# Latent-attention heads: the rotary query channels of two heads in one product

## Chip, core and metric

One NeuronCore of a Trainium2 chip runs the whole kernel. The metric is the device time of one execution in microseconds (us).

## What is computed

One encoder layer over 512 tokens of 2048 channels, in float32: a mixer with two attention branches, then a mixture of 16 experts. The change concerns the latent-attention branch (8 heads). Cut to it:

```python
q = (_rmsnorm(cq, g_cq) @ w_uq).reshape(b, s, MLA_HEADS, MLA_NOPE_DIM + MLA_ROPE_DIM)   # 8 heads x (128 + 64)
qn, qr = q[..., :MLA_NOPE_DIM], _rope(q[..., MLA_NOPE_DIM:], ang_1d)
kv = (_rmsnorm(ckv, g_ckv) @ w_ukv).reshape(b, s, MLA_HEADS, MLA_NOPE_DIM + MLA_V_DIM)
kr = _rope(kr, ang_1d)                                # one rotary key, shared by the heads
s = (einsum(qn, kn) + einsum(qr, kr)) * scale
p = softmax(s);  o = p @ v

def _rope(x, ang):                                    # x1, x2: halves of 32 channels
    return concatenate([x1 * cos - x2 * sin, x1 * sin + x2 * cos])
```

## The kernel before

Engines are programmed separately and meet in semaphores; the order on each engine is written out by hand. Stages, in order: adaLN columns and the combined input projection, the gate projections, **attention** (about 646 to 870 us of the profile), the two branch projections, the output projection, the experts. In attention one loop runs over `i` = 0..7; each turn does latent head `i` and grouped-query head `i+1` (the latter is called attention `2i+2`, latent head `i` is attention `2i+1`; `a` counts both).

Products are exact to float32 by splitting both operands in a rounded part (`_hi`, type fp32r, made by ACT) and a rest (`_lo`, made by DVE): `split_product` (L902) issues hi*hi, lo*hi and hi*lo. A product over the 512-channel latent with 128 output channels and 512 tokens is thus 4 x 3 = 12 matmuls of 512 columns.

Turn `i` on PE (L1002 to L1025): `project(i)` makes the head's rotary queries in bank 5 (12 matmuls), its other queries in bank 4 (12) and its keys in bank 7 (6); on even `i` `values_two` makes the values of two heads in banks 6 and 5, two token tiles in each; on `i` = 3 the second grouped-query key head is transposed into bank 5. Then `rope_scores` (12 matmuls into banks 0 to 3), two transpositions of the probabilities of attention `2i`, `nope_scores` (12 more into the same banks), the transposition of the next grouped-query queries into bank 5, and the rest of attention `2i` and, between its parts, the scores of attention `2i+2` and the values of `2i+1`.

The rotary queries of one head take 128 columns because each of its 64 channels is wanted twice: the weights stand as [q1 q2 | q2 q1] (`uq` is 256 wide, `wq` is loaded with two extra strips of 32 columns, L580 and L581), the table `qtab` holds [cos cos -sin sin], one multiplication on DVE over 128 rows (L2106) turns the bank, and the keys stand twice under one another (`kr2`, L1994), so that the product over 128 rows adds the two halves.

```python
for b, w0, turn in ((5, P, 1), (4, 0, 2)):            # L918: rotary queries, then the others
    split_product(bank[b][:, :], by_k(4, lambda k: three(uq_hi[:, k, w0:w0 + P], ...)), True, True)
k[:, C_QTAB:C_QTAB + S] = np.concatenate([c1.T, c1.T, -s1.T, s1.T])   # L103
```

ACT's turn: the copy of the previous latent head's output (`output_hi`), `head_inputs(i)` (L1591: `qr_hi`, `qn_hi`, `kn_hi`, on even `i` the values), the weights of head `i+1` (`head_uq_hi`, `head_ukv_hi`), three exponentials, `item_hi`, the fourth, the normalisation of the probabilities (L1583), and the same for attention `2i+2`. DVE's turn: `output_lo`, `head_rests(i)` (L2103: the turning, then `qr_lo`, `qn_lo`, `kn_lo`), the weight rests, the copies `pT` of transposed probabilities (L2101) with the negative maxima of the scores (L2082, L2084) between them. `inverse_sums` waits for the four exponentials. On `i` = 7 the next head's weights are replaced by the first two chunks of the branch weights (`hi(N_BR, 0)`, `hi(N_BR + 1, 1)` on ACT, L1622, and `lo` on DVE, L2129); these use the memory that holds `uq`, `uk` and `uv` during attention.

The SP queue loads the head weights (L578): four transfers per head, heads 0 and 1 at the start, head `H` as soon as DVE has split head `H-2`. PE's `project(i)` waits for the rests of its weights (`hw_lo`), for `o_lo` before bank 4 and for `pT_ready` before bank 7.

## Time and profile before

| | us |
|---|---|
| median of 3 runs (lowest to highest) | 2217.11 (2216.94 to 2217.76) |
| the profiled execution, device time | 2216.92 |
| its span, first to last instruction | 2214.6 |
| attention in it, first scores to first branch product | 646.5 to 869.5 |

The span leaves out some 2.3 us around the program. PE is TensorE's matmuls, PEld its weight loads, DVE VectorE, ACT ScalarE, SP the queue that issues the loads. A matmul row merges matmuls of one kind that follow each other; as they are pipelined, the distance of two rows' starts, not the row's length, is what the first costs. In brackets stands the idle time before a row and who ended it.

### The profile page before, as it was taken

The page shows a single profiled execution, that of the slowest core. Times are in us where ns is not written, and L with a number is a line of the kernel's source. Part 1 is how long each engine was busy: PE and PEld are TensorE (multiplying, and loading weights), DVE is VectorE, ACT ScalarE, POOL GpSimd, SP SyncE. Part 2 cuts the span into 40 slices and gives each one's busy share as a digit, 9 for nine tenths or more (in the row PEclk, how much of TensorE's full clock was granted, in tenths as well). Part 3 has the DMA queues.
Part 4 walks back from the last instruction along what each step waited for, and adds up shares of the span by engine and source line. Part 5 has one row for each costly group of instructions (what it writes and reads, how often), then busy time and mean ns, then how long its engine had stood idle before and what let it go on. Part 6 is the DMA issues. An engine that isn't in the chain of part 4 may idle for free.

```text
span 2214.6 us, 26365 instructions
## 1 busy us (share of the span) xinstructions
PE 2124.1 (96%) x10338; PEld 1380.8 (62%) x10338; DVE 871.9 (39%) x1229; ACT 566.4 (26%) x996; POOL 4.7 (0%) x8
## 2 busy tenths in 40 slices
PE   7999999999999999999999899999999999998996
PEld 4777788888887767888888545343534444444432
DVE  4572667666666665445433400202030202121114
ACT  4254442222246664212222511010100000100102
POOL 0000000000000000000000000000000000000000
PEclk9999999999999999999999999999999999999999
DMA  9966775888770100543422699999999999999998
GB/s 335 338 228 248 270 252 169 319 314 288 276 236 26 29 15 1 190 154 130 158 94 76 273 390 425 390 427 427 426 428 429 426 428 426 428 427 426 427 423 309
DMA packets 150319, 635.61 MB, mean 287 GB/s; under 512 B 20418, under 2 KB 33880, under 8 KB 119012
## 3 DMA queue, kind: packets, MB, share of 16 engines
q1 hardware_dynamic: 145636, 626.18, 72.0%
q10 hardware_dynamic: 4608, 8.39, 1.0%
q8 instruction: 52, 0.85, 0.2%
q14 instruction: 23, 0.19, 0.0%
HBM read 621.94 MB, written 12.58 MB: 287 GB/s over the span
## 4 chain that ended last, share of the span: by engine, by line
PE 84%; DMA 8%; DVE 4%; ACT 1%; SPq 1%; issue 1%; DVEq 0%; ACTq 0%
PE bank L1219 25%; PE bank L744 24%; PE bank L746 13%; DMA e_wide<-in_w_e_up 6%; PE bank L1191 5%; PE bank L905 4%; PE bank L794 3%; PE bank L991 2%; PE bank L1211 2%; PE bank L1212 1%; DMA e_slot<-in_w_e_down 1%; PE bank L1201 1%; PE bank L713 1%; PE bank L979 1%; DMA sh_tile<-in_w_ada 1%
## 5 line engine op out<-in xcount | busy, mean ns | idle before, releaser
L1219 PE MATMUL bank<-e_wide,xgT 128*64 128x512 f32 x1456 | 405.5, 603 | 42.8 <-DMA e_slot<-in_w_e_up 16.3
L1398 ACT ACTIVATE w_hi<-stage 128x1024 fp32r<-128x1024 f32 (+1 forms) x168 | 175.3, 1044 | 600.7 <-PE bank L744 339.9
L1801 DVE TENSOR_TENSOR w_lo<-stage,w_hi 128x1024 fp32r<-128x1024 f32 (+1 forms) x168 | 202.4, 1205 | 313.9 <-ACT w_hi L1398 313.2
L1219 PEld LDWEIGHTS bank<-e_wide,xgT 128*64 128x64 f32 x1456 | 129.0, 139 | 292.1 <-issue 289.6
L1219 PE MATMUL bank<-e_slot,xgT 128*64 128x512 f32 x584 | 213.1, 610 | 0.0
L1219 PE MATMUL bank<-e_wide,heT 128*64 128x512 f32 x672 | 168.7, 595 | 0.0
L744 PE MATMUL bank<-hT_hi,w_hi 128*128 128x512 f32 x512 | 159.2, 392 | 0.0
L744 PE MATMUL bank<-hT_lo,w_hi 128*128 128x512 f32 x512 | 158.0, 390 | 0.0
L744 PE MATMUL bank<-hT_hi,w_lo 128*128 128x512 f32 x512 | 157.8, 389 | 0.0
L1872 DVE SCALAR_TENSOR_TENSOR ada_acc<-ada_tile,siluc,ada_acc 128x1024 f32<-128x1024 f32 x116 | 148.7, 1282 | 6.7 <-DMA ada_tile<-in_w_ada 1.2
L2334 DVE TENSOR_TENSOR x<-x,bank 128x512 f32<-128x512 f32 x128 | 79.6, 683 | 175.3 <-PE bank L1212 173.8
L2324 DVE SCALAR_TENSOR_TENSOR y<-bank,val,gt_row 128x512 f32<-128x512 f32 x32 | 22.0, 745 | 318.4 <-PE bank L1219 318.4
L1723 ACT ACTIVATE xgT<-bank,modcol,a 128x128 f32<-128x128 f32 x112 | 42.1, 456 | 402.7 <-PE bank L1191 402.7
L1219 PEld LDWEIGHTS bank<-e_wide,heT 128*64 128x64 f32 x672 | 52.9, 137 | 101.5 <-issue 99.4
L1191 PEld LDWEIGHTS bank<-sel,xn 128*128 128x128 f32 x896 | 102.3, 192 | 17.0 <-issue 17.0
L744 PEld LDWEIGHTS bank<-hT_lo,w_hi 128*128 128x128 f32 x512 | 96.1, 188 | 20.2
L744 PEld LDWEIGHTS bank<-hT_hi,w_lo 128*128 128x128 f32 x512 | 96.1, 188 | 20.2
L744 PEld LDWEIGHTS bank<-hT_hi,w_hi 128*128 128x128 f32 x512 | 95.1, 188 | 18.9
L1191 PE MATMUL bank<-sel,xn 128*128 128x128 f32 x896 | 106.8, 278 | 0.0
L1219 PE MATMUL bank<-e_slot,heT 128*64 128x512 f32 x328 | 95.7, 595 | 2.8 <-DMA e_slot<-in_w_e_down 2.0
L2368 DVE TENSOR_TENSOR sg<-bank,sg 128x512 f32<-128x512 f32 x16 | 10.3, 686 | 199.8 <-PE bank L1219 199.8
L1219 PEld LDWEIGHTS bank<-e_slot,xgT 128*64 128x64 f32 x584 | 63.9, 140 | 32.8 <-issue 32.0
(346 smaller groups left out, 2979.7 us busy)
## 6 DMA issues: line engine op xcount, KB each, us to landing
e_wide<-in_w_e_up SPq DMA_DIRECT2D x49, 2048.0 KB, 16.0
e_wide<-in_w_e_gate SPq DMA_DIRECT2D x42, 2048.0 KB, 13.6
e_wide<-in_w_e_down SPq DMA_DIRECT2D x42, 2048.0 KB, 17.3
ada_tile<-in_w_ada SPq DMA_DIRECT2D x160, 512.0 KB, 5.5
stage<-in_w_in SPq DMA_DIRECT2D x96, 512.0 KB, 6.4
e_slot<-in_w_e_gate SPq DMA_DIRECT2D x43, 1024.0 KB, 15.5
e_slot<-in_w_e_down SPq DMA_DIRECT2D x41, 1024.0 KB, 16.9
e_slot<-in_w_e_up SPq DMA_DIRECT2D x30, 1024.0 KB, 10.6
```

The lines of the kernel that those rows point to most:

```text
L744: last = mm(bank[b][:, :], w[:, s, kk, b * P:(b + 1) * P], a[:, k, :], start=first, stop=end)
L746: last = mm(bank[b][:, :], a[:, k, b * P:(b + 1) * P], w[:, s, kk, :], start=first, stop=end)
L794: last = mm(acc, a[:, 2 * cc + kk, b * P:(b + 1) * P], w[:, s, kk, w0:w1], start=first, stop=end)
L905: last = mm(acc, stationary, moving, start=start and n == 0, stop=stop and n == len(operands) - 1)
L991: mm(bank[4][:, :], v, pT[:, kt % 2, :], start=kt == 0, stop=kt == 3).then_inc(pv_done, 1)
L1191: last = mm(bank[b][:, i * P:(i + 1) * P], xn[:, t, (4 * u + i) * P:(4 * u + i + 1) * P], sel[:, t, :, :], start=t == 0, stop=t == T - 1)
L1211: mm(bank[4 + t][:, :], selT[:, t * P:(t + 1) * P], y_hi[jd % 2][:, :], start=True, stop=False)
L1219: last = mm(acc[h][64 * e:64 * e + 64, :], stationary(e), weights(h, e), start=first, stop=end)
L1398: A(w_hi[:, c % NSPLIT, :, 0:width], stage[:, c % NSTAGE, :, 0:width], ACT.Copy).then_inc(hi_ready, 1)
L1801: V.tensor_tensor(w_lo[:, c % NSPLIT, :, 0:width], stage[:, c % NSTAGE, :, 0:width], w_hi[:, c % NSPLIT, :, 0:width].bitcast(F32), ALU.sub ...
L1872: V.scalar_tensor_tensor(out_acc, tile, siluc[:, k:k + 1], acc, ALU.mult, ALU.add).then_inc(ada_done, 1)
L2334: V.tensor_tensor(x1[:, t, jd * W:(jd + 1) * W], x1[:, t, jd * W:(jd + 1) * W], bank[4 + t][:, :], ALU.add).then_inc(scat_added, 1)
```

## The change

The rotary channels of an even head and the odd head after it form one stationary operand of 128 columns (`uqr`, 64 + 64), and `project` makes them in one product, on even `i` alone. Odd heads make only their other queries, now in bank 5, and their keys. The bank then holds 64 rows of each head, each channel once. Four multiplications on DVE over 64 rows and 512 columns turn them: head `i` times cosine and times sine into the two halves of `q_rot` (in SBUF), then head `i+1` times cosine into the lower and times sine into the upper rows of bank 5. The sine rows no longer carry the swap of halves or the sign: the keys do, `kr2` is [k1 k2 | k2 -k1] with k the turned key. `qr_hi`/`qr_lo` are made from `q_rot`, and `qr2_hi`/`qr2_lo` from bank 5 for the odd head, in the memory of `uqr`. The odd head's rotary scores read those.

What moves with it: the weights of a head are two transfers, not four (`wq` is 192 wide); one transfer of 256 KB loads the sine table `q_sin` after those of head 1; `uqr` is split on ACT and DVE on odd turns for the next pair (ACT after the first block of scores of head `i` is done, since `qr2` lies there), for the first pair before anything else; `q_rot` and `qr2` are split on even turns. On turn 7 the first branch chunk waits for the first block of scores, and the second stands between the third and the fourth exponential.

```diff
@@ constants
-    k[:, C_QTAB:C_QTAB + S] = np.concatenate([c1.T, c1.T, -s1.T, s1.T])
+    k[:, C_QTAB:C_QTAB + S] = np.concatenate([c1.T] * 4)
+    k[:, C_QSIN:C_END] = np.concatenate([s1.T] * 4)
@@ head_weights, on SP
-                sp.dma_start(wq[:, b, :, 0:192], w_uq_v[:, :, ds(H * 192, 192)]).then_inc(hw_full[b], 16)
-                sp.dma_start(wq[:, b, :, 192:224], w_uq_v[:, :, ds(H * 192 + 160, 32)]).then_inc(hw_full[b], 16)
-                sp.dma_start(wq[:, b, :, 224:256], w_uq_v[:, :, ds(H * 192 + 128, 32)]).then_inc(hw_full[b], 16)
+                sp.dma_start(wq[:, b, :, :], w_uq_v[:, :, ds(H * 192, 192)]).then_inc(hw_full[b], 16)
...
+                if H == 1:
+                    sp.wait_ge(pro_done, 7)
+                    sp.dma_start(q_sin[:, :], consts[:, C_QSIN:C_END]).then_inc(consts_in, 16)
@@ project, on PE
-                pe.wait_ge(hw_lo, weights_split(i) + 1)
-                for b, w0, turn in ((5, P, 1), (4, 0, 2)):
-                    if turn == 2 and i:
+                if i % 2 == 0:
+                    pe.wait_ge(hw_lo, split_of(i, "uqr"))
+                    split_product(bank[5][:, :], by_k(4, lambda k: three(uqr_hi[:, k, :, :], uqr_lo[:, k, :, :], cqT_hi[:, k, :], cqT_lo[:, k, :])),
+                                  True, True).then_inc(proj_done, 1)
+                    if i:
                         pe.wait_ge(o_lo, 2 * i)
-                    split_product(bank[b][:, :], by_k(4, lambda k: three(uq_hi[:, k, w0:w0 + P], uq_lo[:, k, w0:w0 + P],
+                pe.wait_ge(hw_lo, split_of(i, "uq"))
+                split_product(query_bank(i), by_k(4, lambda k: three(uq_hi[:, k, :], uq_lo[:, k, :], cqT_hi[:, k, :], cqT_lo[:, k, :])),
+                              True, True).then_inc(proj_done, 1)
@@ values_two, on PE: before the third token tile, which goes to bank 5
-                        pe.wait_ge(proj_lo, 4 * i + 2)
+                        pe.wait_ge(proj_lo, rests(i) + 4)
@@ turn 3, on PE: before the transposition into bank 5
-                    pe.wait_ge(proj_lo, 4 * i + 2)
+                    pe.wait_ge(proj_lo, rests(i) + 1)
@@ head_uqr_hi, on ACT
+                act.wait_ge(hw_full[1], 32 * (H // 2 + 1))
+                if H:
+                    act.wait_ge(s_done, 4 * (2 * H - 1) + 1)
+                else:
+                    act.wait_ge(hw_full[0], 32)
+                    act.wait_ge(chunk_used, N_BR + 1)
+                A(uqr_hi[:, :, :, :].rearrange("p k e n -> p e k n"), wq[:, :, :, P:P + ROPE], ACT.Copy).then_inc(hw_hi, 1)
@@ turn 7, on ACT
-                    act.wait_ge(proj_done, 4 * HM)
+                    act.wait_ge(s_done, 4 * (2 * i + 1) + 1)
                     hi(N_BR, 0)
-                    hi(N_BR + 1, 1)
...
                 exponentials(2 * i + 1, 12, range(3))
...
+                else:
+                    hi(N_BR + 1, 1)
@@ head_rests, on DVE
-                V.tensor_tensor(bank[5][:, :], bank[5][:, :], qtab[:, :], ALU.mult).then_inc(proj_lo, 1)
+                if i % 2 == 0:
+                    a, b = slice(0, ROPE), slice(ROPE, 2 * ROPE)
+                    dve.wait_ge(proj_done, projected(i) + 1)
+                    V.tensor_tensor(q_rot[a, :], bank[5][a, :], qtab[a, :], ALU.mult)
+                    V.tensor_tensor(q_rot[b, :], bank[5][a, :], q_sin[a, :], ALU.mult).then_inc(proj_lo, 1)
+                    dve.wait_ge(proj_lo, n + 1)
+                    V.tensor_tensor(bank[5][a, :], bank[5][b, :], qtab[b, :], ALU.mult)
+                    V.tensor_tensor(bank[5][b, :], bank[5][b, :], q_sin[b, :], ALU.mult).then_inc(proj_lo, 1)
...
+                    V.tensor_tensor(qr_lo[:, :], q_rot[:, :], qr_hi[:, :].bitcast(F32), ALU.subtract).then_inc(proj_lo, 1)
+                    dve.wait_ge(proj_hi, n + 2)
+                    V.tensor_tensor(qr2_lo[:, :], bank[5][:, :], qr2_hi[:, :].bitcast(F32), ALU.subtract).then_inc(proj_lo, 1)
@@ before the first turn, on DVE
+            dve.wait_ge(consts_in, 16 * 3)
+            head_uqr_lo(0)
             head_uq_lo(0)
```

Three places show the order. PE, the start of turn 1 (an odd head), before:

```order
L905 MATMUL bank5<-cqT_hi_185,uq_hi_197 128x512 x4
L905 MATMUL bank5<-cqT_hi_185,uq_lo_198 128x512 x4
L905 MATMUL bank5<-cqT_lo_186,uq_hi_197 128x512 x4
L905 MATMUL bank4<-cqT_hi_185,uq_hi_197 128x512 x4
L905 MATMUL bank4<-cqT_hi_185,uq_lo_198 128x512 x4
L905 MATMUL bank4<-cqT_lo_186,uq_hi_197 128x512 x4
L905 MATMUL bank7<-ckvT_hi_187,uk_hi_201 128x512 x2
```

and now:

```order
L919 MATMUL bank5<-cqT_hi_187,uq_hi_199 128x512 x4
L919 MATMUL bank5<-cqT_hi_187,uq_lo_200 128x512 x4
L919 MATMUL bank5<-cqT_lo_188,uq_hi_199 128x512 x4
L919 MATMUL bank7<-ckvT_hi_189,uk_hi_207 128x512 x2
L919 MATMUL bank7<-ckvT_hi_189,uk_lo_208 128x512 x2
L919 MATMUL bank7<-ckvT_lo_190,uk_hi_207 128x512 x2
L919 MATMUL bank0<-krT_hi_191,qr2_hi_203 128x512
```

Twelve matmuls are gone from the turn; bank 5 now holds the other queries, and the rotary scores read `qr2`. DVE, the start of turn 2 (an even head), before:

```order
L2089 TENSOR_TENSOR oT_lo_86<-bank4,oT_hi_85 128x512
L2106 TENSOR_TENSOR bank5<-bank5,qtab_211 128x512
L2110 TENSOR_TENSOR qr_lo_66<-bank5,qr_hi_65 128x512
L2112 TENSOR_TENSOR qn_lo_64<-bank4,qn_hi_63 128x512
L2114 TENSOR_TENSOR kn_lo_196<-bank7,kn_hi_195 128x512
L2034 TENSOR_TENSOR uq_lo_198<-wq_61,uq_hi_197 128x1024
```

and now:

```order
L2134 TENSOR_TENSOR oT_lo_87<-bank4,oT_hi_86 128x512
L2154 TENSOR_TENSOR q_rot_62<-bank5,qtab_217 64x512
L2155 TENSOR_TENSOR q_rot_62<-bank5,q_sin_185 64x512
L2157 TENSOR_TENSOR bank5<-bank5,qtab_217 64x512
L2158 TENSOR_TENSOR bank5<-bank5,q_sin_185 64x512
L2162 TENSOR_TENSOR qr_lo_67<-q_rot_62,qr_hi_66 128x512
L2164 TENSOR_TENSOR qr2_lo_204<-bank5,qr2_hi_203 128x512
L2167 TENSOR_TENSOR qn_lo_65<-bank4,qn_hi_64 128x512
L2169 TENSOR_TENSOR kn_lo_198<-bank7,kn_hi_197 128x512
L2073 TENSOR_TENSOR uq_lo_200<-wq_61,uq_hi_199 128x512
```

Four instructions more stand ahead of `qn_lo` and `kn_lo`, and the split of the next head's weights is half as wide. ACT, turn 7, before:

```order
L1600 ACTIVATE kn_hi_195<-bank7 128x512
L1398 ACTIVATE w_hi_50<-stage_49 128x1024 x2
L1576 ACTIVATE probs_m_184,rsum_226<-bank0,nmax_225,zr_223 128x512
L1576 ACTIVATE probs_m_184,rsum_226<-bank1,nmax_225,zr_223 128x512
L1576 ACTIVATE probs_m_184,rsum_226<-bank2,nmax_225,zr_223 128x512
L1576 ACTIVATE probs_m_184,rsum_226<-bank3,nmax_225,zr_223 128x512
```

and now:

```order
L1635 ACTIVATE kn_hi_197<-bank7 128x512
L1419 ACTIVATE w_hi_50<-stage_49 128x1024
L1607 ACTIVATE probs_m_186,rsum_232<-bank0,nmax_231,zr_229 128x512
L1607 ACTIVATE probs_m_186,rsum_232<-bank1,nmax_231,zr_229 128x512
L1607 ACTIVATE probs_m_186,rsum_232<-bank2,nmax_231,zr_229 128x512
L1419 ACTIVATE w_hi_50<-stage_49 128x1024
L1607 ACTIVATE probs_m_186,rsum_232<-bank3,nmax_231,zr_229 128x512
```

One of the two copies of branch weights has gone behind the third exponential.

## Rows read from the trace of the kernel before

**Rows 1.** the page, part 1 (busy time) and part 4 (the chain that ended last).

```profile
span 2214.6 us, 26365 instructions
...
PE 2124.1 (96%) x10338; PEld 1380.8 (62%) x10338; DVE 871.9 (39%) x1229; ACT 566.4 (26%) x996; POOL 4.7 (0%) x8
...
PE 84%; DMA 8%; DVE 4%; ACT 1%; SPq 1%; issue 1%; DVEq 0%; ACTq 0%
```

**Rows 2.** busy time of each engine, clock and DMA, in turns 1 and 2.

```profile
678.88:706.24 27.36, 26.93 (x120) 18.83 (x119) 18.61 (x36) 16.90 (x34) 0.00 (x0) 1.00 0.11 30
706.24:736.15 29.91, 29.77 (x144) 21.71 (x143) 18.05 (x35) 17.57 (x35) 0.00 (x0) 1.00 0.10 27
```

**Rows 3.** waits of PE alone, window 640:885 us: total, times, longest.

```profile
PE bank L991 <- DVE pT L2101: 1.1, 4, 0.3
```

**Rows 4.** timeline of PE, turn 1: start us, us, line, operands.

```profile
678.88 1.49 PE L905 MATMUL bank<-cqT_hi,uq_hi 128*128 128x512 f32 x4
...
682.02 1.07 PE L905 MATMUL bank<-cqT_hi,uq_hi 128*128 128x512 f32 x4
...
684.75 0.61 PE L905 MATMUL bank<-ckvT_hi,uk_hi 128*128 128x512 f32 x2
...
686.10 0.39 PE L905 MATMUL bank<-krT_hi,qr_hi 128*128 128x512 f32 x1
...
689.62 0.48 PE L905 MATMUL bank<-kn_hi,qn_hi 128*128 128x512 f32 x1
...
696.79 1.12 PE L991 MATMUL bank<-pT,zg 128*128 128x512 f32 x2 [0.29 <-DVE pT L2101]
```

**Rows 5.** timeline of ACT and DVE, turn 1.

```profile
677.70 2.56 ACT L1583 ACTIVATE probs_g<-probs_g,rsum 128x512 f32<-128x512 f32 x4 [0.25 <-DVE rsum L2094]
...
692.13 0.78 ACT L1576 ACTIVATE probs_m<-bank,nmax,zr 128x512 f32<-128x512 f32 x1 [3.46 <-DVE nmax L2084]
...
687.88 1.23 DVE L2034 TENSOR_TENSOR uq_lo<-wq,uq_hi 128x1024 fp32r<-128x1024 f32 x1 [0.26 <-ACT uq_hi L1524]
689.03 0.42 DVE L2039 TENSOR_TENSOR uk_lo<-wkv,uk_hi 128x256 fp32r<-128x256 f32 x1
...
698.65 0.69 DVE L2082 TENSOR_REDUCE nmax<-bank 128x1 f32<-128x512 f32 x1 [1.91 <-PE bank L905]
```

**Rows 6.** timeline of DVE, ACT and PE, turn 2.

```profile
709.59 0.70 DVE L2106 TENSOR_TENSOR bank<-bank,qtab 128x512 f32<-128x512 f32 x1 [0.76 <-PE bank L905]
...
710.33 0.60 ACT L1594 ACTIVATE qr_hi<-bank 128x512 fp32r<-128x512 f32 x1 [2.22 <-DVE bank L2106]
...
718.12 1.22 DVE L2034 TENSOR_TENSOR uq_lo<-wq,uq_hi 128x1024 fp32r<-128x1024 f32 x1 [3.13 <-ACT uq_hi L1524]
...
714.90 0.40 PE L905 MATMUL bank<-uv_hi,ckvT_hi 128*128 128x256 f32 x2
```

**Rows 7.** timeline of ACT, DVE and PE, before turn 0.

```profile
646.06 1.06 ACT L1524 ACTIVATE uq_hi<-wq 128x1024 fp32r<-128x1024 f32 x1 [0.47 <-ACT sig L1555]
...
649.23 0.63 ACT L1533 ACTIVATE uv_hi<-wkv 128x512 fp32r<-128x512 f32 x1 [1.80 <-DMA wkv<-in_w_ukv]
...
646.68 0.17 DVE L1876 TENSOR_TENSOR modcol<-bank,bcol 128x8 f32<-128x8 f32 x1 [5.65 <-PE bank L713]
...
649.37 1.07 PE L905 MATMUL bank<-cqT_hi,uq_hi 128*128 128x512 f32 x4
```

**Rows 8.** DMA of 640:642 us, then of 646:648 us: packets in the window.

```profile
DMA packets 1499, 0.49 MB, mean 246 GB/s; under 512 B 1044, under 2 KB 1499, under 8 KB 1499
...
DMA packets 824, 0.77 MB, mean 384 GB/s; under 512 B 363, under 2 KB 573, under 8 KB 824
```

**Rows 9.** timeline of ACT, DVE and PE, turn 7 and the start of the branch products.

```profile
859.18 2.00 ACT L1398 ACTIVATE w_hi<-stage 128x1024 fp32r<-128x1024 f32 x2
...
860.27 2.36 DVE L1801 TENSOR_TENSOR w_lo<-stage,w_hi 128x1024 fp32r<-128x1024 f32 x2 [0.26 <-ACT w_hi L1398]
...
867.86 2.23 PE L991 MATMUL bank<-pT,zg 128*128 128x512 f32 x4 [0.25 <-DVE pT L2101]
```

118 lines of the change are left out of this document (72 added, 46 removed).

## The prediction

> **What bounds the kernel now.** I read the page first, for what kind of work fills the end's path: TensorE is busy for 96% of the span and is 84% of the chain that ended last [rows 1]. So a matmul taken away is worth its time wherever PE has nothing to wait for, and the question is whether attention is such a place. The busy time by turn says so: of 27.36 us PE is busy for 26.93 in turn 1, of 29.91 for 29.77 in turn 2, while DVE and ACT are at 17 to 19 and the clock is granted in full [rows 2]. The waits of PE confirm it: 1.1 us in four waits over the whole stage, the longest 0.3, all in `times_v` for a copy `pT` from DVE [rows 3]. The odd turns have one each, 0.29 us in turn 1 [rows 4]. That wait matters: it says that a second chain (keys, weight splits, maxima, exponentials, sums, `pT`) is only just behind PE in odd turns, so PE's gain is real only if this chain comes earlier by as much.
>
> **What is removed.** Twelve matmuls from each odd turn. In turn 1 the second product of twelve starts at 682.02 and what follows it at 684.75, so one product costs 2.73 us; no wait stands in it [rows 4]. Four odd turns make 4 x 2.73 = 10.9 us. On even turns PE issues the same numbers of matmuls with the same columns as before; the rotary product's 128 columns merely belong to two heads. That is 0.
>
> **Does the second chain follow in turns 1, 3 and 5?** I write times from the start of the turn (678.88), before: keys begin at 5.87, rotary scores at 7.22, the other scores at 10.74, and the waited-for `times_v` starts at 17.91 [rows 4]. Now the keys end at 4.5, rotary scores at 7.2, and the other scores begin at 8.0. ACT's normalisation of the probabilities that are transposed then ended at 680.26, thus at 1.4: no new wait [rows 5]. On DVE `kn_lo` now ends near 6.0 and the weight splits follow: `uq_lo` was 1.23 for 1024 elements [rows 5] and is now about 0.69 for 512 (as the multiplication over 512, 0.70 [rows 6]), the two others 0.4 and 0.7; they end near 7.6, before the first transposition is complete at 7.9. Two copies of some 0.6 bring the first maximum to 9.1, when the first block of scores (at 8.9) is there. Before, the first exponential stood at 692.13, 2.5 us behind the start of the scores [rows 4, 5]; now 2.1. So the chain moves by 2.73 + 0.4, and PE's wait shrinks a little: I book 0.1 x 3 = 0.3 gained. The new ACT copy `uqr_hi` (512 elements, 0.63 like `uv_hi` [rows 7]) waits for that first block, fits in the 3.46 us in which ACT waited for maxima, and ends at 9.7, before the first exponential at 10.1. `uqr_lo` (0.69) fits in the 1.91 us in which DVE waited for scores [rows 5]. If this cover were gone, each would cost its own length, 4 us in all over three turns.
>
> In turn 3 the key transposition into bank 5 now waits for `qn_lo`, which reads that bank. It is reached one product and the keys after the start, and `qn_lo` follows its product by 0.2 + 0.60 (ACT) + 0.70 (DVE) = 1.5 us against 1.36 us of keys: a wait of 0.1 to 0.3 us. I take 0.25; it uses up the 0.3.
>
> **Turn 7** differs. Before, two branch chunks were split before the scores: 2.00 us on ACT, 2.36 on DVE, which kept DVE until 862.6 [rows 9]. Now DVE is free when the transposed probabilities come, and the maxima start 0.6 earlier against the scores (the two copies, 1.2 us, no longer begin at 862.6 but while PE transposes), but the second ACT copy (1.0 us, half of 2.00) stands ahead of the fourth exponential, and `inverse_sums`, then the last `pT`, wait for that. The chain gets 0.4 longer against PE, at the one place where PE already waited 0.25 [rows 9]. Cost: 0.4 to 0.5. The bound from below is 0 (if the copy fits between maxima), from above 1.0. I take 0.5.
>
> **Even turns: the turning.** One DVE multiplication of 0.70 becomes four over 64 rows and as many elements per row. Nearest rows: 0.70 for 128 rows x 512 elements [rows 6]. I take 0.70 each. From 709.59: four make 712.4; ACT copies bank 5 until 713.1; `qr2_lo` ends at 713.8. PE wants bank 5 for the third token tile, at 714.90 [rows 6]: slack 1.0 us, cost 0. `qn_lo` and `kn_lo` come about 0.7 later than before, and PE wants them only behind all four value tiles; `uq_lo` had waited 3.13 us for ACT [rows 6]. Bounds: 0.35 each if half the rows cost half (nothing gained, PE does not wait there), 1.2 each if they cost as 1024 elements [rows 6]: then 2.0 us longer, 1.0 us of waiting, 4 us over the four turns.
>
> DVE instructions that follow each other without a wait overlap by some 0.1 us: `uq_lo` of turn 1 runs from 687.88 to 689.11, `uk_lo` starts at 689.03 [rows 5]. The Trainium skill, "VectorE: DVE Perf Modes", section "Two Vector instructions with no wait between them", holds an instruction back whose rows start in another group of 32 than those before, which these four do. By it the four lose that overlap, some 0.4 us; with the full 0.70 each that I used, this is inside the slack, and it speaks for the rival on the turning, not for the sum.
>
> **Before turn 0.** ACT first splits `uqr` for both heads, so it needs head 1's weights now at about 646.0, and DVE needs `q_sin`. Before, the last of head 1's four transfers released ACT only at 649.23, while PE was to begin the projection at 649.37 [rows 7]. That would cost: ACT 0.63 and DVE 0.69 from 649.2 on put the first product at 650.7, 1.3 us late, and DVE, now that much behind, would make bank 5 free 1.5 us late in the values: 2.8 us. What speaks against it: about the same bytes (1.53 MB with `q_sin`, 1.54 before), but without the four transfers of 128-byte pieces; with these in flight the engines moved 246 GB/s at full share with 1044 of 1499 packets under 512 B, later 384 GB/s with 363 of 824 [rows 8]. At a rate between, 1.53 MB issued from 638.3 on are there near 645 to 646. I take 0. The upper bound is 2.8; the lower is 0, since PE is busy until 649.37 anyway.
>
> The Trainium skill, "DMA: Bandwidth & Descriptors", section "Specifications", wants transfers of at least 512 B for line rate, with a read-modify-write below. The rows above agree in direction (246 against 384 GB/s); by it the weights come sooner still, which supports the 0.
>
> **After attention** nothing is tied to an earlier clock: branch weights wait for buffers, gate values for the last output, expert weights for products. PE's chain continues directly from the last `times_v`, so what attention gives up arrives whole. Row lengths there and the DMA share stay.
>
> **The sum.** 10.9 + 0.3 - 0.25 - 0.5 = 10.45. The profiled execution took 2216.92, so 2206.5; the median of the runs stands 0.2 higher, which gives **2206.6** (-0.5%). Two runs can be told apart from about 0.2%, 4.4 us, on.
>
> **The rivals.**
> - *Late first weights*: head 1's weights or `q_sin` land after 646.9 and PE waits before turn 0. For: ACT waited for just them, 1.80 us [rows 7]. Against: fewer, larger packets. 2206.6 plus up to 2.8, about 2208.5. Chance 0.12.
> - *The turning overruns its slack*: halves over shifted rows cost more than 0.70, PE waits in the values of even turns. With 1.2 each, 4 us: 2210.6; with 1.0 each 2207.4. Chance 0.08.
> - *The second chain does not follow*: the wait for `pT` in odd turns grows by what PE saves. For: it exists today, in four places [rows 3]. Against: its work begins with the keys and scores, which come earlier. Gain then only what was under no wait; say a quarter of 10.9, 2214. Chance 0.05.
> - *Slower*: the four half-row multiplications, of which two shift rows, cost about 2.0 us each. Then bank 5 is free 5.2 us later than I reckon, PE waits 4.2 us in each even turn, 17 in all: 2206.6 + 17 = 2223.6. It decides from about 1.6 us each, where the waits eat the 10.5. Nothing in the rows is so slow per element. Chance 0.03.
> - *It doesn't do what it says*: the order on PE shows the twelve matmuls gone from each odd turn, so this is out.
>
> The forecast's own case keeps 0.72. Its width comes from turn 7 (0 to 1.0), the waits in turns 1, 3, 5 (0 to 0.9 recovered) and turn 3: 2205.2 to 2207.6. Most of the first two rivals is to be held too, so the range is 2204.9 to 2210.4. Faster by over 0.2%: forecast, late weights, most of the turning, 0.92; within 0.2%: 0.05; slower: 0.03.
>
> **What would show it.** PE's matmul count 48 lower. Turn 1 shorter by 2.7 to 2.9 (27.36 to about 24.6), turn 2 at 29.9 as before, attention 10.4 shorter; from the first branch product to the end no difference. Four 64-row rows of near 0.70 at the start of even turns, no PE wait before the third token tile. First product of turn 0 at 649.4. In turn 7 a PE wait of 0.6 to 0.8 before the last `times_v`. A PE wait over 0.5 us in the values, before turn 0, or at every odd `pT`, proves me wrong at that step.

## The result, and the profile after

| | before | changed |
|---|---|---|
| median of 6 runs each (us) | 2217.44 | 2206.57 |
| lowest to highest | 2216.6 to 2218.12 | 2204.95 to 2207.06 |
| profiled execution, device time | 2216.92 | 2206.36 |
| its span | 2214.6 | 2204.6 |

The ratio is 0.995, 95% interval 0.994 to 0.996: faster by 0.5%. The forecast was 2206.6.

The page, parts 1 and 4, answers to [rows 1]: 48 matmuls fewer.

```profile
span 2204.6 us, 26278 instructions
...
PE 2114.4 (96%) x10290; PEld 1372.6 (62%) x10290; DVE 874.3 (40%) x1241; ACT 565.1 (26%) x1000; POOL 4.7 (0%) x8
...
PE 85%; DMA 9%; DVE 3%; SPq 1%; issue 1%; ACT 1%; DVEq 0%; ACTq 0%
```

Windows over turns 1 and 2 (start and end, length, busy time of PE, PEld, DVE, ACT and POOL, granted clock, DMA share, GB/s), against [rows 2]: turn 1 is 3.07 us shorter, turn 2 has its old length.

```profile
679.48:703.77 24.29, 24.15 (x109) 16.57 (x107) 17.22 (x35) 16.52 (x34) 0.00 (x0) 1.00 0.09 28
703.77:733.71 29.94, 29.79 (x144) 21.69 (x143) 20.09 (x39) 17.67 (x36) 0.00 (x0) 1.00 0.08 23
```

The waits of PE in the whole of attention, against [rows 3]: the four of 0.3 us have become one of 0.7.

```profile
PE bank L1012 <- DVE pT L2146: 0.7, 1, 0.7
```

All turns, from the start of one projection to the next (turn 7 to the first branch product), in us:

| turn | 0 | 1 | 2 | 3 | 4 | 5 | 6 | 7 | attention |
|---|---|---|---|---|---|---|---|---|---|
| before | 29.51 | 27.36 | 29.91 | 27.89 | 29.94 | 27.36 | 29.92 | 18.27 | 223.03 |
| changed | 29.51 | 24.29 | 29.94 | 25.03 | 29.89 | 24.27 | 29.93 | 15.73 | 211.46 |

Attention, from the first scores to the first branch product, is 11.57 us shorter; 10.45 had been forecast. The spans differ by 10.0, because the other stages differ by a little: attention began 0.6 us later in this execution, the stretch from the first branch product to the first expert product took 398.07 instead of 397.33 us, the experts 0.2 more. What of that belongs to the change is asked below. The device times differ by 10.56 in the same pair, 0.56 more than the spans: outside the span lie 2.32 us before and 1.76 after. Over all executions on record this rest is 1.8 to 2.5 us for the kernel before and 1.8 to 1.9 for the changed one; no row says why.

Turn 1 on PE: projection, keys, the other scores and the third piece of the second product with the values, which had waited 0.29 us in [rows 4].

```profile
679.48 1.49 PE L919 MATMUL bank<-cqT_hi,uq_hi 128*128 128x512 f32 x4
...
682.63 0.62 PE L919 MATMUL bank<-ckvT_hi,uk_hi 128*128 128x512 f32 x2
...
687.50 0.48 PE L919 MATMUL bank<-kn_hi,qn_hi 128*128 128x512 f32 x1
...
693.36 2.07 PE L1012 MATMUL bank<-pT,zg 128*128 128x512 f32 x4
```

The keys now come 3.15 us after the start of the turn, not 5.87, and the last row has no wait in front of it. DVE in the same turn, against [rows 5]:

```profile
681.38 0.69 DVE L2134 TENSOR_TENSOR oT_lo<-bank,oT_hi 128x512 fp32r<-128x512 f32 x1 [2.52 <-ACT oT_hi L1620]
...
685.43 0.68 DVE L2073 TENSOR_TENSOR uq_lo<-wq,uq_hi 128x512 fp32r<-128x512 f32 x1
...
688.55 0.68 DVE L2127 TENSOR_REDUCE nmax<-bank 128x1 f32<-128x512 f32 x1
...
694.17 0.68 DVE L2078 TENSOR_TENSOR uqr_lo<-wq,uqr_hi 128x512 fp32r<-128x512 f32 x1
```

`uq_lo` took 1.23 before and now 0.68, and the first maximum stands 9.07 us after the start of the turn. The first row will matter most: `oT_lo`, which empties bank 4, ends 2.59 us into the turn. At this point PE is in bank 5 and does not care.

The turning of turn 2 on DVE, against [rows 6], and PE's third token tile:

```profile
707.12 0.68 DVE L2154 TENSOR_TENSOR q_rot<-bank,qtab 64x512 f32<-64x512 f32 x1 [0.77 <-PE bank L919]
707.82 0.68 DVE L2155 TENSOR_TENSOR q_rot<-bank,q_sin 64x512 f32<-64x512 f32 x1
708.54 0.70 DVE L2157 TENSOR_TENSOR bank<-bank,qtab 64x512 f32<-64x512 f32 x1
709.25 0.71 DVE L2158 TENSOR_TENSOR bank<-bank,q_sin 64x512 f32<-64x512 f32 x1
...
710.71 0.69 DVE L2164 TENSOR_TENSOR qr_lo<-bank,qr_hi 128x512 fp32r<-128x512 f32 x1
711.32 0.68 DVE L2167 TENSOR_TENSOR qn_lo<-bank,qn_hi 128x512 fp32r<-128x512 f32 x1
711.92 0.68 DVE L2169 TENSOR_TENSOR kn_lo<-bank,kn_hi 128x512 fp32r<-128x512 f32 x1
```

```profile
712.43 0.40 PE L919 MATMUL bank<-uv_hi,ckvT_hi 128*128 128x256 f32 x2
```

Half the rows cost what all cost. The four start 0.70 to 0.72 us apart, while `qn_lo` and `kn_lo`, as long, start 0.60 apart: the halves do lose the overlap of 0.1 us. Between the second and the third the program itself makes DVE wait (`dve.wait_ge(proj_lo, n + 1)`), so that distance, 0.72, says nothing; the two others, 0.70 and 0.71, have no such wait. That agrees with what the Trainium skill says in "VectorE: DVE Perf Modes", section "Two Vector instructions with no wait between them". `qr2_lo` (its row prints the memory's other name) ends at 711.40, PE wants the bank at 712.43: slack 1.03.

ACT at the start, against [rows 7]: the weights are there in time.

```profile
646.69 0.63 ACT L1555 ACTIVATE uqr_hi<-wq 128x512 fp32r<-128x512 f32 x1 [0.49 <-ACT sig L1586]
```

ACT was released by its own work, not by a transfer: the last weights of head 1 were issued at 640.42 and landed 5.3 us later, 1.0 ahead of this row. The DMA packets of 640:642, against [rows 8]: 16 short ones, where there had been 1044; the rate is no higher, 236 GB/s against 246.

```profile
DMA packets 605, 0.47 MB, mean 236 GB/s; under 512 B 16, under 2 KB 605, under 8 KB 605
```

Turn 7 on ACT and the end of it on PE, against [rows 9]:

```profile
855.34 1.04 ACT L1419 ACTIVATE w_hi<-stage 128x1024 fp32r<-128x1024 f32 x1
856.28 0.77 ACT L1607 ACTIVATE probs_m<-bank,nmax,zr 128x512 f32<-128x512 f32 x1
```

```profile
858.00 1.13 PE L1012 MATMUL bank<-pT,zg 128*128 128x512 f32 x2 [0.67 <-DVE pT L2146]
```

### The profile page after: what moved, and what is told of

Its sections match the earlier page's. It is cut to its first block, busy times and chain, and to the rows that moved or that the text cites. A ratio compares the mean times of both kernels' runs of the same rounds, so it can differ in the third digit from the quotient of the medians.

```text
span 2204.6 us, 26278 instructions
## 1 busy us (share of the span) xinstructions
PE 2114.4 (96%) x10290; PEld 1372.6 (62%) x10290; DVE 874.3 (40%) x1241; ACT 565.1 (26%) x1000; POOL 4.7 (0%) x8
## 4 chain that ended last, share of the span: by engine, by line
PE 85%; DMA 9%; DVE 3%; SPq 1%; issue 1%; ACT 1%; DVEq 0%; ACTq 0%
PE bank L1240 25%; PE bank L758 24%; PE bank L760 13%; DMA e_wide<-in_w_e_up 7%; PE bank L1212 5%; PE bank L919 5%; PE bank L1012 3%; PE bank L808 3%; PE bank L1232 2%; PE bank L1233 1%; PE bank L1000 1%; DMA e_slot<-in_w_e_down 1%; PE bank L1222 1%; PE bank L727 1%; DMA sh_tile<-in_w_ada 1%
## 5 line engine op out<-in xcount | busy, mean ns | idle before, releaser
L1419 ACT ACTIVATE w_hi<-stage 128x1024 fp32r<-128x1024 f32 (+1 forms) x168 | 175.4, 1044 | 604.7 <-PE bank L758 339.9
```

Source lines behind the costliest of these rows:

```text
L1419: A(w_hi[:, c % NSPLIT, :, 0:width], stage[:, c % NSTAGE, :, 0:width], ACT.Copy).then_inc(hi_ready, 1)
```

## The experiments

There are twelve experiments; the last two are the changed kernel and the kernel before once more. The executions of one kernel scatter by 2 to 8 us, more than the smaller effects in question, and a part of that is that the stages before attention differ from one execution to the next: over the fourteen profiled executions of this study the first scores stood at 644.2 to 649.1 us. The lengths of turns and of attention are steadier (the changed kernel twice: 211.46 and 211.53), so the verdicts rest on them, with the medians beside them.

### The product put back

```diff
+                if i % 2:
+                    split_product(query_bank(i), by_k(4, lambda k: three(uq_hi[:, k, :], uq_lo[:, k, :], cqT_hi[:, k, :], cqT_lo[:, k, :])),
+                                  True, True)
                 split_product(query_bank(i), by_k(4, lambda k: three(uq_hi[:, k, :], ...
```

> The changed kernel with the query product of odd turns made twice, into the same bank one after the other: twelve matmuls are put back on TensorE in turns 1, 3, 5 and 7 and nothing else. Theory (TensorE bounds the odd turns and every matmul counts): 4 x 2.73 = 10.9 us slower than the change, but the waits that odd turns had before do not return, since the narrower splits stay: about 2217.5 us, turn 1 at 24.29 + 2.73 = 27.0 us, the matmuls 48 more. Rival (the second chain of odd turns, shortened by the narrower weight splits and the moved copies, is what gave most of the gain): the added product hides in part, less than half of 10.9 us comes back, below 2212 us, with turn 1 below 25.6 us.

Measured: 2216.33 us, ratio to before 0.9997 (0.9988 to 1.0007). Turn 1 27.02, turn 3 27.77, turn 5 27.03, attention 222.37. The only wait of PE in attention is that of turn 7:

```profile
865.99 1.12 PE L1015 MATMUL bank<-pT,zg 128*128 128x512 f32 x2 [0.71 <-DVE pT L2149]
```

So the 48 matmuls are worth 222.37 - 211.53 = 10.84 us, all of their length, and the rival falls. What is left to the kernel before, with as many matmuls, is 223.03 - 222.37 = 0.66 us, 0.34 of it in turn 1.

### The kernel before, without most of the product

Here the rotary product of odd heads is one matmul of its twelve; eleven partial products are left out, so its result is not the layer's. It shows what the matmuls alone are worth.

```diff
-                    split_product(bank[b][:, :], by_k(4, ...), True, True).then_inc(proj_done, 1)
+                    parts = by_k(4, lambda k: three(uq_hi[:, k, w0:w0 + P], uq_lo[:, k, w0:w0 + P], cqT_hi[:, k, :], cqT_lo[:, k, :]))
+                    if b == 5 and i % 2:
+                        parts = parts[:1]
+                    split_product(bank[b][:, :], parts, True, True).then_inc(proj_done, 1)
```

> The kernel before, in which the rotary product of odd turns is one matmul of its twelve; it leaves out eleven partial products of the rotary queries of odd heads. Queues, splits, transfers and waits stay. Theory (the removed matmuls are the gain): 4 x 11 x 0.2275 = 10.0 us faster than before, 2207.4 us, turn 1 at 24.9 us, with a wait for pT near 0.3 us as before, since the chain of DVE starts from the keys and moves along. Rival (the second chain does not follow, because its wide weight splits stay as they were): the wait for pT in odd turns grows to over 1.5 us, the gain stays under 5 us, above 2212 us. Between the two: the amount by which turn 1 is longer than 24.3 + 0.23 us is what narrower splits and moved work gave in the change.

Measured: 2219.44 us, ratio to before 1.0009 (0.9999 to 1.0018); attention 226.33, 3.3 us longer than before. It gained nothing, and neither theory had said why. The `pT` waits are as before, as the theory has it (0.27 in turn 1), so the second chain did follow. The time went to a place that none had named. PE at the start of turn 1:

```profile
678.31 0.80 PE L905 MATMUL bank<-cqT_hi,uq_hi 128*128 128x512 f32 x1
680.95 1.32 PE L905 MATMUL bank<-cqT_hi,uq_hi 128*128 128x512 f32 x4 [1.85 <-DVE oT_lo L2091]
...
685.39 0.63 PE L905 MATMUL bank<-ckvT_hi,uk_hi 128*128 128x512 f32 x2
```

The other queries go to bank 4, which holds the output of the attention before until DVE has read it in `oT_lo`. In the kernel before the rotary product lay over that wait: it began with the turn, lasted 3.14 us [rows 4], and `oT_lo` was done at 681.47, 0.55 us before its end. DVE in turn 1 of the kernel before:

```profile
680.78 0.69 DVE L2089 TENSOR_TENSOR oT_lo<-bank,oT_hi 128x512 fp32r<-128x512 f32 x1 [2.52 <-ACT oT_hi L1589]
```

Without the product PE waits. And the wait costs more than itself: the twelve matmuls behind take 685.39 - 680.95 = 4.44 us instead of 2.73, since the clock was down. The windows show it (the seventh number is the clock):

```profile
680.00:682.00 2.00, 1.05 (x4) 0.89 (x5) 1.30 (x2) 0.64 (x2) 0.00 (x0) 0.97 0.00 0
682.00:684.00 2.00, 2.00 (x6) 1.56 (x5) 0.69 (x1) 0.13 (x1) 0.00 (x0) 0.50 0.00 0
```

0.50 is the lower of the two levels, 1.2 GHz. Turn 1 is 28.60 us, longer than the 27.36 of the kernel that does more. The changed kernel escapes this by a part of the diff that had seemed a detail: on odd turns `query_bank` is bank 5.

### Bank 4 in odd turns

The theory formed from that run, tested by undoing the bank alone:

```diff
             def query_bank(i):
-                return bank[4 + i % 2][:, :]
+                return bank[4][:, :]
...
-                    if i:
-                        pe.wait_ge(o_lo, 2 * i)
+                if i:
+                    pe.wait_ge(o_lo, 2 * i)
```

(`qn_hi` and `qn_lo` read bank 4 accordingly.)

> The changed kernel with the query product of odd turns made in bank 4, as on even turns, instead of bank 5. Bank 4 still holds the output of the turn before, so the product waits for oT_lo. Nothing else differs; the same matmuls run. Theory (formed from the run in which the kernel before was robbed of eleven matmuls and gained nothing: the removed product was also cover for that wait, and only the other bank makes its removal worth anything): in turn 1 oT_lo ends 2.6 us behind the start of the turn, TensorE waits 2.5 us there, its granted clock falls for the products behind as it did in that run, 1.7 us more: turn 1 at 28.4 us instead of 24.29, four times 4 us, 2222 us, slower than the kernel before. Rival (the product that was taken away is a gain of its own and the bank a detail): turn 1 under 26 us, below 2212 us in all.

Measured: 2217.56 us, ratio to before 1.0006 (0.9997 to 1.0015); attention 224.06, 1.0 longer than in the kernel before. The same matmuls in the same order as in the change, and nothing of its gain is left. The waits come where they were expected, 2.12 us long and not 2.5, and one turn in two pays for the clock behind them. Turn 1 and turn 3 on PE:

```profile
681.03 1.16 PE L919 MATMUL bank<-cqT_hi,uq_hi 128*128 128x512 f32 x4 [2.12 <-issue]
...
737.64 2.05 PE L919 MATMUL bank<-cqT_hi,uq_hi 128*128 128x512 f32 x4 [2.13 <-issue]
```

The wait stands in front of an odd turn's first row and so counts in the length of the turn before; hence pairs. Against the change, turns 0 and 1 together are 2.4 us longer, 2 and 3 3.9, 4 and 5 2.4, 6 and 7 3.9. I had expected the fall in all four, 16 us; it came in two, and the bank is worth 224.06 - 211.46 = 12.6 us. The releaser reads "issue" here, but PE starts at 681.03, 0.10 us behind the end of DVE's `oT_lo`:

```profile
680.24 0.69 DVE L2134 TENSOR_TENSOR oT_lo<-bank,oT_hi 128x512 fp32r<-128x512 f32 x1 [2.51 <-ACT oT_hi L1620]
```

The edit and the next run say the same.

### Bank 4, and the cover back

On top of the experiment before:

```diff
+                if i % 2:
+                    pe.wait_ge(hw_lo, split_of(i, "uq"))
+                    split_product(bank[5][:, :], by_k(4, ... the query product once before, into bank 5
                 if i:
                     pe.wait_ge(o_lo, 2 * i)
```

> The kernel with bank 4 in odd turns once more, and in front of its query product the same twelve matmuls once before, into bank 5, where nothing waits: 48 matmuls more than the change, as many as before. Theory (the product that the change removed was the cover of the wait for oT_lo): no wait for oT_lo is left, turns 0 and 1 together 29.5 + 27.0 us, attention 222.4 us and thus 1.7 us shorter than in the run with bank 4 alone (224.06), although TensorE does 10.9 us more work; in all 2216 to 2217 us. Rival (the wait is for something else and comes on top): attention 224.06 + 10.9 = 235 us, 2228 us.

Measured: 2216.88 us, ratio to before 0.9997 (0.9987 to 1.0006); turns 0 and 1 29.50 + 27.03, attention 222.41, no wait of PE in attention but the 0.7 us of turn 7.

Ten microseconds and more of useless matmuls in front of the wait make attention 1.65 us shorter. The product that the change took away was cover.

### DVE's chain longer again

```diff
                 dve.wait_ge(hw_hi, split_of(H, "uq"))
+                if H % 2 == 0 and H:
+                    link(V.tensor_tensor(uq_lo[:, :, :], wq[:, H % 2, :, 0:P], uq_hi[:, :, :].bitcast(F32), ALU.subtract))
```

on top of the first experiment (`link` makes the next instruction wait for this one).

> The changed kernel with the second query product of odd turns put back, as in the first experiment, and DVE's uq_lo in turns 1, 3 and 5 made twice, 0.68 us more on DVE ahead of the first transposed probabilities (the wide split before cost 1.23, the narrow one 0.68, so 0.55 more before). Theory (the narrower splits are what took the wait of 0.3 us out of odd turns): TensorE waits some 0.3 to 0.45 us for pT in turns 1, 3 and 5 again, turn 1 is 27.3 to 27.5 us instead of 27.02, attention 223.3 to 223.7 instead of 222.37. Rival (something else in the change shortened DVE's chain, and the split ends in an idle stretch): no wait, turn 1 at 27.0 us.

Measured: 2218.6 us (2214.07 to 2222.22); turns 1, 3 and 5 at 27.22, 27.95 and 27.24, attention 223.04. Turn 1 is 0.20 longer than without the second `uq_lo`; that is less than the 0.3 to 0.45 expected, and no single wait is long enough to be listed. So a longer DVE split explains 0.20 of the 0.34 us by which the first experiment's turn 1 is shorter than that of the kernel before. The other 0.14 this run could not bring back, for it lengthens DVE's half of the split and leaves ACT's narrow: `uq_hi` takes 0.62 us in it, and took 1.06 in turn 1 of the kernel before, where DVE waited 0.26 for it ahead of `uq_lo` [rows 5]. The first maximum stands 11.81 us behind the start of the turn in the first experiment, 12.12 here and 12.28 before, so the missing 0.14 of the turn lies beside 0.16 on DVE. No run tests ACT's part by itself.

### The turning made longer

```diff
-                    V.tensor_tensor(q_rot[a, :], bank[5][a, :], qtab[a, :], ALU.mult)
+                    link(V.tensor_tensor(q_rot[a, :], bank[5][a, :], qtab[a, :], ALU.mult))
+                    link(V.tensor_tensor(q_rot[b, :], bank[5][a, :], q_sin[a, :], ALU.mult))
+                    V.tensor_tensor(q_rot[a, :], bank[5][a, :], qtab[a, :], ALU.mult)
```

> The changed kernel with two more multiplications over 64 rows at the head of the turning in even turns, each waited for before the next begins: 2 x 0.70 us and some 0.1 us for each of these waits, 1.4 to 1.6 us longer until bank 5 is free. Theory (the turning has a slack of about 1.0 us in turns 2, 4 and 6): TensorE waits 0.4 to 0.6 us before the third token tile in each even turn, and turn 0, where DVE starts the turning earlier against it or not, somewhat alike: 1.6 to 2.4 us slower, near 2208.6 us, turn 2 at 30.4 us. Rival (no slack, DVE's turning is as long as TensorE's cover): 5.6 us or more, 2212 us. Second rival (slack over 1.6 us): nothing, 2206.6 us.

Measured: 2206.8 us (2206.16 to 2208.09); turns 0, 2, 4 and 6 at 30.19, 30.49, 30.50 and 30.45, attention 2.4 us longer than in the change, at the upper end of what was expected of it; the median moved by less. PE in turn 2:

```profile
714.17 0.50 PE L919 MATMUL bank<-uv_hi,ckvT_hi 128*128 128x256 f32 x2 [0.30 <-DVE qr_lo L2166]
```

The rest that sets bank 5 free ends 1.46 us later in the turn and the turn is 0.55 longer: a slack of 0.9, where the rows gave 1.03. Both rivals fall. Turn 0 is 0.68 longer, which makes its slack 0.8; DVE comes to it straight from splitting the weights of the values.

### The rest of the rotary weights, where DVE is wanted

```diff
                 probs_transposed(2 * i, 1)
+                if i % 2 and i < HM - 1:
+                    head_uqr_lo(i + 1)
                 negative_max(2 * i + 1, 12, range(4))
...
-                elif i % 2:
-                    head_uqr_lo(i + 1)
```

> The changed kernel with DVE's rest of the rotary weights (uqr_lo, 0.68 us) of turns 1, 3 and 5 moved from behind the second product with the values to ahead of the second block of maxima (those of the group-attention heads), in the stretch where DVE is wanted. Theory (its place in a stretch where DVE waits is what makes it free; here it stands on the chain of the odd turn): DVE's chain from there on is 0.7 us later in three turns, and TensorE, whose wait for pT has gone but with little to spare, waits 0.3 to 0.7 us in each: 1 to 2 us slower, 2207.6 to 2208.6 us. Rival (DVE has room everywhere in odd turns): no difference, 2206.6 us, no wait over 0.2 us for pT in turn 1.

Measured: 2210.15 us (2208.88 to 2213.84); turns 1, 3 and 5 at 25.45, 26.17 and 25.43, attention 214.93, 3.5 us longer. The direction is right, the size was too small: 1.15 us in each turn, not 0.3 to 0.7. DVE in turn 1 says why:

```profile
689.80 0.69 DVE L2078 TENSOR_TENSOR uqr_lo<-wq,uqr_hi 128x512 fp32r<-128x512 f32 x1 [0.57 <-ACT uqr_hi L1555]
690.41 0.68 DVE L2127 TENSOR_REDUCE nmax<-bank 128x1 f32<-128x512 f32 x1
```

DVE stood still for 0.57 us in front of the moved instruction, until ACT had made `uqr_hi`. The first maximum is 10.35 us behind the start of the turn, not 9.07, and PE waits twice:

```profile
694.54 1.12 PE L1012 MATMUL bank<-pT,zg 128*128 128x512 f32 x2 [0.42 <-DVE pT L2146]
696.05 1.12 PE L1012 MATMUL bank<-pT,zg 128*128 128x512 f32 x2 [0.38 <-DVE pT L2146]
```

So the added weight split is free by its place, and the margin of odd turns is small: 1.28 us more on DVE, 1.16 in the turn.

### The second branch copy later

```diff
                     item_hi(QUERY[i + 1])
-                else:
-                    hi(N_BR + 1, 1)
...
                 output_hi(2 * i)
+                if i == HM - 1:
+                    hi(N_BR + 1, 1)
```

> The changed kernel with ACT's copy of the second branch chunk in turn 7 moved from ahead of the fourth exponential of the last item to behind the copy of its output. Theory (this copy of 1.04 us is what puts the last pT late): TensorE's one wait in attention, 0.67 us for pT in turn 7, goes, turn 7 is 15.1 us instead of 15.73, in all 0.6 to 0.7 us faster than the change, 2205.9 us, which would beat both kernels. Rival (the copy is wanted by the first branch products just as much): the wait moves to the first branch products, no gain, 2206.6 us.

Measured: 2204.37 us (2203.54 to 2207.2), ratio to before 0.9944 (0.993 to 0.9957); the change beside it on the same chip 2206.94. Turn 7 is 14.98 us, attention 210.68, and PE waits nowhere in it. The last two products with the values and the first branch product:

```profile
857.04 2.07 PE L1012 MATMUL bank<-pT,zg 128*128 128x512 f32 x4
858.55 0.79 PE L758 MATMUL bank<-oT_hi,w_hi 128*128 128x512 f32 x1
```

The wait was due to that copy and went without a successor. By the trace this version beats both kernels, by 0.85 us against the change in attention; the intervals of the whole runs do not separate it from the change.

### The weights in pieces again

```diff
-                sp.dma_start(wq[:, b, :, :], w_uq_v[:, :, ds(H * 192, 192)]).then_inc(hw_full[b], 16)
+                sp.dma_start(wq[:, b, :, 0:128], w_uq_v[:, :, ds(H * 192, 128)]).then_inc(hw_full[b], 16)
+                sp.dma_start(wq[:, b, :, 128:160], w_uq_v[:, :, ds(H * 192 + 128, 32)]).then_inc(hw_full[b], 16)
+                sp.dma_start(wq[:, b, :, 160:192], w_uq_v[:, :, ds(H * 192 + 160, 32)]).then_inc(hw_full[b], 16)
```

(with the counts that ACT waits for.)

> The changed kernel with each head's query weights loaded again by three transfers, two of them in pieces of 128 bytes, so eight more transfers before turn 0 of which four are of short pieces. Theory (the short pieces were what made head 1's weights late, and now the first ACT instruction of attention needs them): the last of head 1's transfers lands near 649.2 us as it did before, ACT's first split begins then and not at 646.7, and TensorE waits 1.3 us before turn 0 and up to 1.5 us in its values: 1.3 to 2.8 us slower, 2208 to 2209.4 us. Rival (the loads have slack whatever their pieces): ACT's first split begins within 0.3 us of what it does in the change, no wait, 2206.6 us.

Measured: 2205.09 us (2203.67 to 2206.93); turn 0 at 30.27 instead of 29.51, all others as in the change, attention 212.32. ACT's first split:

```profile
645.52 0.63 ACT L1557 ACTIVATE uqr_hi<-wq 128x512 fp32r<-128x512 f32 x1 [2.01 <-DMA wkv<-in_w_ukv]
```

PE, third token tile of turn 0:

```profile
656.18 0.51 PE L921 MATMUL bank<-uv_hi,ckvT_hi 128*128 128x256 f32 x2 [0.48 <-DVE qr_lo L2166]
```

This execution began attention at 644.41, so the split stands 1.11 us behind the first scores, against 0.41 ahead of them in the change: 1.5 us later, waiting for a transfer. TensorE did not wait before turn 0, and 0.76 us is all that reached it: less than the expected 1.3 to 2.8, and no loss shows in the median.

But this run holds two causes. It has shorter pieces and it has more transfers, and the SP queue issues them some 0.55 us apart: the last weights of head 1 are issued 3.67 us after the first, against 1.48 in the change.

### As many transfers, long pieces

```diff
-                sp.dma_start(wq[:, b, :, :], w_uq_v[:, :, ds(H * 192, 192)]).then_inc(hw_full[b], 16)
+                sp.dma_start(wq[:, b, 0:2, :], w_uq_v[:, 0:2, ds(H * 192, 192)]).then_inc(hw_full[b], 16)
+                sp.dma_start(wq[:, b, 2:3, :], w_uq_v[:, 2:3, ds(H * 192, 192)]).then_inc(hw_full[b], 16)
+                sp.dma_start(wq[:, b, 3:4, :], w_uq_v[:, 3:4, ds(H * 192, 192)]).then_inc(hw_full[b], 16)
```

> The changed kernel with each head's query weights loaded by three transfers again, as many as in the run in pieces, but split by rows of the channel index, so that every piece has 768 bytes. The run in pieces had two causes in one: pieces of 128 bytes, and four more transfers before turn 0, which the SP queue issues 0.55 us apart, so that the last weights of head 1 were issued 3.7 us after the first and not 1.5. Theory A (the short pieces made them late): ACT's first split is released by its own work, 0.4 us ahead of the first scores, turn 0 29.5 us, as in the change. Theory B (the number of transfers did): the split is released by the weights, about 1.1 us behind the first scores, turn 0 near 30.3 us. In between: both.

Measured: 2206.59 us (2205.37 to 2207.92); turn 0 at 30.12, attention 212.10. ACT's first split, with the first scores at 647.44:

```profile
647.95 0.63 ACT L1557 ACTIVATE uqr_hi<-wq 128x512 fp32r<-128x512 f32 x1 [1.41 <-DMA wkv<-in_w_ukv]
```

It stands 0.51 us behind the first scores, 0.92 later than in the change, where the short pieces made it 1.52; turn 0 is 0.61 longer, where they made it 0.76. So the answer is both, and the number of transfers is the larger part, 0.9 of 1.5 us. The short pieces are left with 0.6.

The landings say it more sharply, since in the change ACT's split is not what the weights release. Counted from the first issue of the head weights, which stands 8.16 us ahead of the first scores in all three, the last weights of head 1 are there after 6.8 us in the change, 8.7 here and 9.3 with the short pieces. The four transfers more cost 1.9 us, all of it issue time (3.37 us from the first to the last issue instead of 1.48), of which 1.0 was slack. The short pieces cost 0.6: 0.3 by issues that take longer (3.67), 0.3 on the way (5.6 us from issue to landing, 5.3 in the two others). "DMA: Bandwidth & Descriptors" in the Trainium skill, section "Specifications", asks for transfers of 512 B and more; the 0.3 us on the way agree with it, and no more than these.

A third cause is in the rows and was not tested by itself. The kernel before had as many transfers, short pieces and us of issuing (3.67) as the run in pieces, yet its last weights took 7.2 us from issue to landing. Up to that transfer it loaded 1536 KB, the run in pieces 1280: the doubled strips, 256 KB, are gone in every version of the change.

### The change again

> The changed kernel once more, beside the others on the same chip. Expected 2206.6 us; turn 1 24.3 us and turn 2 29.9 us. The stages behind attention are the point: if the 0.7 us that the change lost in the top-k stage, where the granted clock rose later, came from the change, the stretch from the first branch product to the first expert product is 398.1 us here too; if it differs from run to run by itself, it lies elsewhere between 397 and 399 us.

Measured: 2206.94 us (2204.93 to 2208.68). Turns 1 and 2 at 24.31 and 29.92, attention 211.53. From the first branch product to the first expert product 397.88 us, thus near the 398.1 that was to show if the loss came with the change. The last section comes back to this number.

### The kernel before again

> The kernel before once more, for one profile. Attention 223.0 us. From the first branch product to the first expert product: 397.3 us as before if that length belongs to the kernel; near 397.9 us if it differs from one execution to the next.

Measured: 2215.7 us in its one execution, the profiled one; attention 223.08, turns 1 and 2 at 27.38 and 29.95, and 397.17 us from the first branch product to the first expert product.

## Why the prediction was right, and where it was not supported

**The time** was 2206.57 against 2206.6, and so close by chance. The sum in attention was 1.1 us too small (11.57 against 10.45); in the profiled pair the stages before and behind gave back 1.6, and 0.56 came from outside the span, neither of which a step had foreseen.

**The removed product**: 4 x 2.73 = 10.9 forecast, 10.84 by the first experiment. But the argument had a hole. "No wait stands in it" is a statement on the removed rows; it says nothing on what the removed rows covered. The prediction checked the chain behind the product (keys, maxima, `pT`) and not the wait of the very next product for bank 4, though it was in the kernel's code, and `oT_lo` ended only 0.55 us before it was needed. Had the change left the bank as it was, every step of the working would have stood as written, and the result would have been 2217.6, no gain. It came true because `query_bank` moves the odd heads' product to bank 5, which the prediction never weighed: at this step it was lucky. In the Trainium skill, "Perfetto Trace Analysis", section "Matmuls" asks that independent groups of matmuls rotate through different banks, so that the emptying of one lies beside the next; here that is 12.6 us, more than the matmuls themselves.

**The second chain of odd turns** follows, as forecast: the first maximum moved by 12.28 - 9.07 = 3.21 us (691.16 - 678.88 before), 0.48 more than PE's 2.73, forecast 0.4. The row of the kernel before:

```profile
691.16 0.68 DVE L2082 TENSOR_REDUCE nmax<-bank 128x1 f32<-128x512 f32 x1
```

But the term was 3 x 0.1 and turns 1 and 5 gained 0.34 and 0.36 beyond the product: a chain ahead by 0.48 removes a wait of 0.29 altogether, not a third of it. With turn 3 (2.86 - 2.73, and 0.21 for the wait named below, 0.34) the term comes to 1.04, not 0.3: this is the one that was mis-sized most.

**Turn 3**: 0.25 forecast for the key transposition that waits for `qn_lo`. Turn 3 gained 2.86, 0.2 less than turn 1: right. The rows on PE agree: from the last row of the keys to the transposition there were 0.46 us before (742.94 to 743.40) and are 0.67 now (737.77 to 738.44).

**Turn 7**: forecast a wait of 0.6 to 0.8 and a cost of 0.5. The wait is 0.67, the cost 0.19 (2.73 - 2.54). The version with the later branch copy shows the place without any wait, 14.98 us; measured on that, turn 7 had 18.27 - 2.73 - 14.98 = 0.56 of loss before, though its bracket said 0.25, and has 0.75 now. I had set the new bracket against the old one; if the 14.98 may be used for the kernel before too, which no run shows, the old wait cost twice its bracket. So this term was off by 0.3.

**Even turns**: cost 0, slack 1.0. The slack read after is 1.03, and 0.9 by experiment. The halves take 0.68 to 0.71 each, 0.70 as booked; the rival on them and the slow one are refuted.

**Before turn 0**: cost 0, since the weights come sooner without short pieces. Right, but the reason given, fewer short pieces and by them a rate between 246 and 384 GB/s, is not what the rows show: the rate was 236, and the short pieces are 0.6 us of the landing. More came from four transfers fewer in the SP queue ahead of the last one wanted, 1.9 us, which the prediction had read from no row. The weights did land at 645.7, within the 645 to 646 it gave, but by another sum. It also took the bytes to be about the same, with `q_sin` among them; but `q_sin` is issued behind the weights, and ahead of the last of these 256 KB fewer are loaded. The bound of 2.8 was for a landing as late as before, which no run brought back; 1.52 us later cost 0.76.

**After attention**: "what attention gives up arrives whole". The profiled spans differ by 10.0, the medians by 10.9, where attention gave 11.57. 0.7 us of the difference are in the top-k stage, where the clock rose later; how far by the change is open (last section). The time at which attention begins differs by itself: 646.5 and 645.5 in the kernel before, 647.1 and 646.1 in the change.

## What to carry to other kernels

Before booking a removed piece of work as gained, ask what it covers: look up what the next instruction on its engine waits for, and when that was fulfilled. A resource that was ready 0.55 us before it was needed is a new wait as soon as more than that is removed in front. And a bracket of idle time is not the price of a wait; the length of the turn with and without it is. Here brackets of 0.30, 0.37 and 0.48 us went with turns 0.55, 0.61 and 0.76 longer, and one of 0.67 with 0.75.
